# One product of the RWKV groups, written by GpSimd in place of VectorE

## The reference, cut to what matters

```python
r, k, v = xr @ w_r, xk @ w_k, xv @ w_v
w = -softplus(-(w0 + tanh(xw @ w1) @ w2)) - 0.5
a = sigmoid(a0 + (xa @ a1) @ a2)
kk = heads(k * k_k); kk = kk / max(norm(kk), 1e-12)
k = k * (1.0 + (a - 1.0) * k_a)
# scan over time, per head, with decay = exp(-exp(w)):
#   sa = state @ (-kk)
#   state = state * decay + sa * (kk * a) + v * k
#   o = state @ r
```

## Time and profile before

| what | value |
|---|---|
| median of 3 runs | 940.07 us (939.35 to 941.81) |
| profiled execution, its own time | 941.57 us |
| its span, first to last instruction | 939.8 us |
| TensorE (PE) busy | 922.6 us, 98% of the span |
| VectorE (DVE) busy | 694.6 us, 74% |
| ScalarE (ACT) busy | 489.6 us, 52% |
| GpSimd (POOL) busy | 102.3 us, 11% |
| granted TensorE clock | 0.998 of 2.4 GHz |

### The profile page before, as it was taken

One profiled execution on the slowest core, in us unless ns is written; L12 is line 12 of the kernel. 1 busy time (PEld: TensorE's weight loads), 2 busy tenths in 40 slices (PEclk: granted clock), 3 DMA queues, 4 the chain that ended last, 5 costly groups with the idle time before them and its releaser, 6 DMA issues.

```text
span 939.8 us, 18277 instructions
## 1 busy us (share of the span) xinstructions
PE 922.6 (98%) x7008; PEld 817.0 (87%) x7008; DVE 694.6 (74%) x1286; ACT 489.6 (52%) x786; POOL 102.3 (11%) x78
## 2 busy tenths in 40 slices
PE   9999999999999999999999999999999999999998
PEld 7779789798879888888899999999998798888887
DVE  7888887878656766666697889888878666666665
ACT  4543444334334544445467777777677454455442
POOL 0111100101011000000031133213221000000000
PEclk9999999999999999999999999999999999999999
DMA  9321212201516676666369545544554256676661
GB/s 289 134 65 46 90 59 90 94 11 53 152 45 182 188 209 183 186 200 206 106 207 296 152 134 160 155 144 139 165 157 113 70 145 194 197 201 182 194 181 46
DMA packets 195242, 136.77 MB, mean 146 GB/s; under 512 B 7390, under 2 KB 186078, under 8 KB 195052
## 3 DMA queue, kind: packets, MB, share of 16 engines
q1 hardware_dynamic: 194748, 135.18, 48.3%
q10 hardware_dynamic: 432, 0.72, 0.2%
HBM read 134.83 MB, written 1.05 MB: 145 GB/s over the span
## 4 chain that ended last, share of the span: by engine, by line
PE 88%; DVE 7%; ACT 2%; issue 1%; DMA 1%; POOL 0%; SPq 0%; DVEq 0%; ACTq 0%
PE bank L487 50%; PE wide L487 34%; DVE work L1475 3%; DVE work L1782 1%; ACT work L1088 1%; DMA rows<-in_rows 1%; PE wide L1031 1%; PE bank L1031 1%; ACT L1088 1%; DVE work L1478 1%; DVE x L1475 1%; PE wide L1008 0%; PE bank L1008 0%; ACT Vs L1088 0%; PE bank L510 0%
## 5 line engine op out<-in xcount | busy, mean ns | idle before, releaser
L487 PE MATMUL bank<-wpj,hkq 128*128 128x384 f32 x1152 | 215.3, 340 | 1.5 <-ACT Vs L1088 0.4
L487 PEld LDWEIGHTS bank<-wpj,hkq 128*128 128x128 f32 x1152 | 197.3, 188 | 6.1 <-issue 4.2
L487 PE MATMUL wide<-hsp,wsp 128*128 128x256 f32 (+2 forms) x1120 | 196.2, 328 | 0.0
L487 PEld LDWEIGHTS wide<-hsp,wsp 128*128 128x128 f32 x1120 | 172.4, 190 | 22.5 <-DVE hsp L1475 0.6
L1475 DVE TENSOR_TENSOR wsp<-ring,wsp 128x1024 fp32r<-128x1024 f32 (+1 forms) x88 | 150.7, 1752 | 4.2 <-ACT wsp L1088 4.2
L1088 ACT ACTIVATE wsp<-ring 128x1024 fp32r<-128x1024 f32 (+1 forms) x88 | 130.5, 1485 | 21.7 <-PE wide L487 11.8
L1088 ACT ACTIVATE rows<-wide 128x256 f32<-128x256 f32 x66 | 25.3, 384 | 151.2 <-PE wide L487 151.2
L2077 POOL TENSOR_TENSOR gsm<-gsm,mhalf 128x6 f32<-128x6 f32 (+1 forms) x40 | 74.3, 1876 | 263.9 <-DVE gsm L1995 173.9
L487 PE MATMUL bank<-wsp,asp 128*128 128x512 f32 x396 | 98.2, 392 | 0.0
L1475 DVE TENSOR_TENSOR wpj<-ring,wpj 128x1536 fp32r<-128x1536 f32 x48 | 84.1, 1753 | 17.0 <-ACT wpj L1088 17.0
L487 PEld LDWEIGHTS bank<-wsp,asp 128*128 128x128 f32 x396 | 71.7, 189 | 13.2
(11 more groups left out here) (287 smaller groups left out, 1366.1 us busy)
## 6 DMA issues: line engine op xcount, KB each, us to landing
ring<-in_f_w_gu SPq DMA_DIRECT2D x88, 512.0 KB, 5.9
ring<-in_w_kv SPq DMA_DIRECT2D x96, 256.0 KB, 3.4
ring<-in_f_w_down SPq DMA_DIRECT2D x44, 512.0 KB, 3.7
ring<-in_b_w_q SPq DMA_DIRECT2D x48, 256.0 KB, 3.4
wmix<-in_a_w_k SPq DMA_DIRECT2D x4, 1024.0 KB, 5.3
wmix<-in_a_w_r SPq DMA_DIRECT2D x4, 1024.0 KB, 5.6
wmix<-in_a_w_v SPq DMA_DIRECT2D x4, 1024.0 KB, 5.2
wmix<-in_a_w_o SPq DMA_DIRECT2D x4, 1024.0 KB, 5.3
```

What stands on the lines that cost most here:

```text
L487: return pe.matmul(o, a, b, start=start, stop=stop)
```

## The change

In groups 1 to 3 the product `kP` leaves VectorE's list and enters GpSimd's. GpSimd waits for the keys (`dve_kT`, a new semaphore that `kT_` counts up) and for `En` (`act_E`), and counts up `pool_kP` when it is done. TensorE waits for `pool_kP` beside `dve_scaled`. Group 0 keeps `kP` on VectorE. The semaphore `dve_mhalf` is folded into `dve_ones`.

```diff
@@ TensorE, group
                 pe.wait_ge(S("dve_scaled"), it + 1)
+                if behind:
+                    pe.wait_ge(S("pool_kP"), it)
@@ VectorE, start
-            dve.memset(mhalf[:, :], -0.5).then_inc(S("dve_mhalf"), 1)
+            dve.memset(mhalf[:, :], -0.5).then_inc(S("dve_ones"), 1)
@@ VectorE, group
-                step(tt(flat(kT_), bank[7], flat(t1), ALU.mult))
+                m = tt(flat(kT_), bank[7], flat(t1), ALU.mult)
+                if behind:
+                    m.then_inc(S("dve_kT"), 1)
+                    dve.wait_ge(S("dve_kT"), it)
+                else:
+                    step(m)
...
                 if behind:
                     gate_output(it)
                     q.mark(dve.tensor_copy(pl[:, :, :], par[:, two, lg:lg + 2]))
-                    decayed_keys()
                     dve.wait_ge(S("act_y_hi"), it)
                     low_part(y_lo[:, :, :], yT[:, :, :], y_hi[:, :, :], "dve_y_lo")
@@ GpSimd
-            pool.wait_ge(S("dve_mhalf"), 1)
+            pool.wait_ge(S("dve_ones"), 2)
...
             for it in range(NGRP):
+                if it > 0:
+                    pool.wait_ge(S("dve_kT"), it)
+                    pool.wait_ge(S("act_E"), it * 3 + 1)
+                    pool.tensor_tensor(kP.rearrange("p n t -> p (n t)"), kT_.rearrange("p n t -> p (n t)"), En, ALU.mult).then_inc(S("pool_kP"), 1)
```

## The result

The median rose from 940.38 us to 944.52 us (8 runs each); the ratio of the runs is 1.0038, with a 95% interval of 1.0026 to 1.0051. The forecast was 942.7 us with a range of 939.8 to 943.9. The direction was right, the stall happened where it was forecast, and the time lies 0.6 us above the range.

A forecast was written before the change was run, and what follows sets the result against it. TensorE waits for VectorE's run from `y_lo` to `bP`, itself waiting for ScalarE's `y_hi`. Removal gains 0, the addition held by GpSimd costs 3 x 0.88 = 2.64 us: 942.7 us from a median of 940.07, range 939.8 to 943.9.

The forecast's parts named there:

- The mechanism: Groups 1 to 3: GpSimd's product holds VectorE's two-SBUF-input addition, delaying `y_hi`, `y_lo` and TensorE, 0.88 us a group.
- filled a hole: VectorE ahead of `y_lo`: it waits for ScalarE's `y_hi` anyway, so removing the 0.69 us product gains 0.
- The wait for `pool_kP`: TensorE ahead of `kP`'s products: GpSimd is done 5 us earlier, so the added wait costs 0.
- (a): Same stall but longer, by waiting for GpSimd's recorded end or a product up to 1.59 us: 3.1 to 3.5 us; chance 0.25.
- (b): VectorE's addition is first and on time; `y_lo` is held instead, 0.19 us late, 0.6 us in all; chance 0.14.
- (c): GpSimd's product runs beside the addition without a collision that matters: 0 us, 940.1 us; chance 0.15.
- (d): At `y_lo`: ScalarE's exponentials and the addition come earlier, so the removal saves up to 1.8 us, 938.3 us; chance 0.04.
- 3 x 0.88 = 2.64 us: Three groups, each with `y_lo` 0.88 us late behind the held addition, and nothing back.
- on the median's footing: Step from the profiled execution's 944.2 us, which lay 1.5 us above the median of 940.07, to a forecast of 942.7 us.

The follow-up runs named there:

- e4: Changed kernel with the product `kP` left out on both engines in groups 1 to 3; 939.49 us beside 939.34 before, ratio 1.0004.
- e2: Changed kernel with GpSimd's product also waiting for `dve_y_lo`, so it runs behind `y_lo`; 940.36 us beside 939.34 before, ratio 1.0003.
- e8: e2 with `gate_output` ahead of `kT_` on VectorE and `y_hi` ahead of `E1` on ScalarE; 938.90 us beside 940.41 before, ratio 0.9979.
- e9: Same order as e8, but `kP` stays on VectorE and GpSimd does nothing new; 940.23 us beside 940.41 before, ratio 0.9990.
- e7: Kernel before, `kP` kept on VectorE, with GpSimd filling a 128x512 tensor with zeros at the changed kernel's time; 941.74 us (one run), group 59.64 us.
- e5: Kernel before, `kP` kept on VectorE, with GpSimd making the same product at the changed kernel's time; 944.25 us beside 940.14 before, ratio 1.0034.
- e6: As e5, but GpSimd copies `kT_` in place of multiplying; 941.57 us (one run) beside 940.14 before, group 59.92 us.
- e3: Changed kernel with GpSimd's product also waiting for `dve_y`, the addition's end; 942.19 us beside 939.34 before, ratio 1.0026.
- e10: Kernel before with 8 idle 128x128 matmuls ahead of `product_o` in groups 1 to 3; 943.29 us beside 939.35 before, ratio 1.0035.
- e11: Changed kernel with 7 idle 128x128 matmuls in TensorE's new idle ahead of `product_o`; 943.64 us beside 939.35 before, ratio 1.0037.

## Why the prediction was right and wrong

The mechanism was right. VectorE's 0.69 us filled a hole (e4: 0.0). GpSimd's product took 1.28 us, forecast 1.29; no row had its size, and that two smaller sizes pointed so well at it is in part luck. It came ahead of the addition and held it, in all three groups; the addition ended 0.54 to 0.55 us after GpSimd's record, forecast 0.53. `y_hi`, `y_lo` and TensorE followed. The wait for `pool_kP` cost nothing (e2). The rivals: (a) did not happen, for the addition was let go 0.14 to 0.15 us before it would have been by waiting for GpSimd's recorded end, and the product was not longer; (b) happened in none of the three groups, though GpSimd came first by 0.07 us only; (c) and (d) did not happen, and e8 and e9 show that (d) named the place rightly: once `y_hi` comes earlier, the removal pays. The rule of the Trainium skill (SBUF — State Buffer, "Who interferes with whom") named the right pair of instructions, and e7 agrees with it on writes; taken literally, blocked until the other's end, it would have put the addition's end 0.14 to 0.15 us later than it was.

It was wrong in two places.

- The term 3 x 0.88 = 2.64 us was mis-sized, if little: it measured 2.8 to 2.9 us. GpSimd started 0.14 us after `En`'s end (99.48 against 98.71 + 0.63 in group 1, 160.06 against 159.29 + 0.63 in group 2), not 0.08 as its affine select does. That is 0.06 of the missing 0.07 us a group.

```profile
98.71 0.63 ACT L1090 ACTIVATE work<-work 128x512 f32<-128x512 f32 x1
```

```profile
99.48 1.28 POOL L2104 TENSOR_TENSOR work<-work 128x512 f32<-128x512 f32 x1 [4.81 <-ACT work L1090]
```

- The step that put the time past the range is the one from the sum to the time, "on the median's footing": it took the median of before, 940.07 us from three executions, as a fixed point, and gave the clock no term. Eight executions put before at 940.38. And executions of the same kernel lie some 2 us apart by the granted clock (939.23 us at full clock, 941.24 at 0.998), so the median depends on how many of them have a lower stretch. The forecast of 942.7 us missed 944.52 by 1.8. Of that 0.3 us is the median of before, 0.2 us the mis-sized term, and the other 1.3 us is left to the clock: 11 of the changed kernel's 13 executions had a lower stretch, 31 of 82 of before. Where the clock was alike the sum held: the prediction's 944.2 us for the profiled execution measured 944.57, and the changed kernel's two executions with the full clock (942.1 and 942.8 us) lie inside the range. The range's upper end held the unknown length of the product, and nothing for the clock.

Why the changed kernel has the lower stretch more often is open: that 2 of 13 executions had the full clock, against 51 of 82, was measured, its cause was not.

## What to carry to other kernels

Before moving work to GpSimd, look at what VectorE does in the very same microsecond: a VectorE instruction with two SBUF inputs is held while GpSimd reads, so the place decides, and one more wait that puts the product beside PSUM readers made it free. Before taking work off an engine, follow the chain to the instruction behind it: if that one waits for a third engine, the time freed is worth nothing until that chain is moved (e4 against e8 and e9). And where some executions of a kernel have a lower clock stretch and others don't, compare executions at the same granted clock, or make the range as wide as that stretch.

## What the runs showed of the hardware

- GpSimd's reading of 128x512 in SBUF lengthened VectorE's two-input addition by 1.07 us (a product, 1.28 us) and 0.39 us (a copy, 0.61 us); a write of 0.53 us by 0.00. GpSimd came first there, and its own times did not change (1.28 beside it, 1.30 beside PSUM readers).
- The hold goes the other way too, where VectorE is first. At 88.7 us of before (timelines of VectorE and GpSimd)

```profile
88.71 1.22 DVE L1475 TENSOR_TENSOR wmix_low<-wmix,w_hi 128x1024 fp32r<-128x1024 f32 x1
88.89 1.92 POOL L2077 TENSOR_TENSOR gsm<-gsm,mhalf 128x4 f32<-128x4 f32 x1 [15.64 <-DVE gsm L1632]
```

  GpSimd's small root took 1.92 us beside a two-input instruction of VectorE that had begun 0.18 us sooner. The next five of its shape took 1.01 to 1.02 us. No run tried this by itself.
- How far ahead GpSimd was made no difference: it began 0.07 to 0.08 us ahead in e5 and e6 and 0.62 us ahead in e3, and each time the held 128x512 instruction of VectorE ended 0.55 us after GpSimd's record. In the kernel before, GpSimd held VectorE even with a start recorded 0.03 us later.
- GpSimd's start after its releaser does not depend on the kind of instruction alone: 0.08 us after ScalarE for an affine select and 0.07 to 0.09 after VectorE for its small roots, which read two SBUF tensors as the product does (88.80 to 88.89), each with one wait ahead of it. At the new place, with two waits ahead, it was 0.14 for the product and for e6's copy, and 0.12 for e7's memset; with three waits, the last for VectorE, it was 0.17 to 0.18 (e2, e3). No run varied the number of waits alone.
- A stretch of TensorE at 1.2 GHz separates executions of one kernel by 1.5 us (e10 against before, two traces) to 2.0 us (medians of before at full clock and at 0.998). It was seen behind 2.2 us of idle at 720 us, but also in group 2 behind busy matmuls (e4, e9), and the same idle was seen without it (e10, e11).
